# The end of a product ahead of the attention beside it, in the mixed units of a two-block transformer

## The reference, cut to what matters

```python
def first_block(x, mem, ...):
    x = x + hybrid_mixer(rmsnorm(x, g_mix), w_in, ...)      # 12 softmax heads and 4 stick-breaking heads
    x = x + memory_cross_attention(rmsnorm(x, g_cross), ...)
    x = x + squared_relu_mlp(rmsnorm(x, g_mlp), w_up, w_down)
    return rmsnorm(x, g_final)

def second_block(x, c, ctx, ...):
    for l in range(2):
        ...                        # latent stream x, and in layer 0 the context stream too:
        q_ctx = qk_heads(z_ctx[..., B_Q:B_K], q_norm_g[l])
        attn_ctx = diff_attention(q_ctx, k_ctx, v_ctx, lam)
        out_ctx = mixer_merge(z_ctx, attn_ctx, ...)   # branches a (spatial gate), b (attention), c (convolution)
        ctx = ctx + cg1 * out_ctx
        ...
```

## Time and profile before

| | us |
|---|---|
| median of 3 runs | 3848.04 (3846.48 to 3850.3) |
| profiled execution, device time | 3857.84 |
| its span, first to last instruction | 3856.0 |
| TensorE busy | 3587.3 (93%), 18826 matmuls |
| VectorE busy | 1574.4 (41%) |
| ScalarE busy | 961.7 (25%) |
| GpSimd busy | 2027.6 (53%) |
| granted TensorE clock, mean | 0.957 |

### The profile page before, as it was taken

The page is one execution under the profiler, slowest core; times in us unless marked ns, Lnnn a source line. Parts: engine busy times, 40 slices in busy tenths (PEclk is TensorE's granted clock), DMA queues, the critical chain, the costliest instruction groups (busy, mean ns, idle before and its releaser), DMA issues.

```text
span 3856.0 us, 47215 instructions
## 1 busy us (share of the span) xinstructions
PE 3587.3 (93%) x18826; PEld 2945.9 (76%) x18826; DVE 1574.4 (41%) x2738; ACT 961.7 (25%) x2038; POOL 2027.6 (53%) x1216
## 2 busy tenths in 40 slices
PE   8898889999899999899998899999999998999999
PEld 6776667787678998778776787888778766787887
DVE  7734442224864221464455313341472554214430
ACT  2134333222201111221244312220121443212210
POOL 4454245564458988745432364665544332465655
PEclk9899789988999999899999999999999999999999
DMA  8532122332664443332111132332322111232322
GB/s 297 169 119 82 49 70 84 110 104 66 219 207 131 143 142 121 119 116 72 66 55 44 55 95 80 94 98 90 108 72 77 55 55 44 71 93 82 97 86 101
DMA packets 109868, 389.26 MB, mean 101 GB/s; under 512 B 12057, under 2 KB 16537, under 8 KB 108242
## 3 DMA queue, kind: packets, MB, share of 16 engines
q1 hardware_dynamic: 89280, 315.10, 25.9%
q10 hardware_dynamic: 20370, 71.13, 5.4%
HBM read 379.86 MB, written 6.32 MB: 100 GB/s over the span
## 4 chain that ended last, share of the span: by engine, by line
PE 79%; DVE 13%; ACT 4%; issue 2%; DMA 1%; POOL 1%; ACTq 0%; DVEq 0%; SPq 0%
PE ps L319 20%; PE ps L321 19%; PE ps L320 19%; PE ps L1351 3%; DVE ada L1822 2%; DVE junk L1822 2%; PE ps L929 2%; PE ps L409 2%; PE ps L410 2%; PE ps L411 2%; PE ps L1363 1%; DVE ps L973 1%; DVE small_d L1408 1%; PE ps L1331 1%; PE ps L1044 1%
## 5 line engine op out<-in xcount | busy, mean ns | idle before, releaser
L2385 POOL CAST whi<-raw 128x1024 fp32r<-128x1024 f32 (+1 forms) x606 | 618.7, 1021 | 1767.8 <-DMA raw<-in_w 1767.2
L2387 POOL TENSOR_TENSOR wlo<-raw,whi 128x1024 fp32r<-128x1024 f32 (+1 forms) x606 | 1420.8, 2345 | 48.5
L319 PE MATMUL ps<-hhi,whi 128*128 128x512 f32 x2056 | 842.9, 410 | 90.9 <-DVE hlo L980 15.2
L320 PE MATMUL ps<-hlo,whi 128*128 128x512 f32 x2056 | 818.0, 398 | 0.0
L321 PE MATMUL ps<-hhi,wlo 128*128 128x512 f32 x2056 | 817.3, 398 | 0.0
L319 PEld LDWEIGHTS ps<-hhi,whi 128*128 128x128 f32 x2056 | 393.8, 192 | 211.3 <-DVE hlo L980 21.2
L320 PEld LDWEIGHTS ps<-hlo,whi 128*128 128x128 f32 x2056 | 395.2, 192 | 86.8 <-issue 6.7
L321 PEld LDWEIGHTS ps<-hhi,wlo 128*128 128x128 f32 x2056 | 393.9, 192 | 87.9
L319 PE MATMUL ps<-chi,whi 128*128 128x256 f32 x864 | 256.4, 297 | 6.6 <-DVE mc_lo L881 4.0
L320 PE MATMUL ps<-clo,whi 128*128 128x256 f32 x864 | 249.3, 289 | 0.0
L321 PE MATMUL ps<-chi,wlo 128*128 128x256 f32 x864 | 248.6, 288 | 0.0
(11 more groups left out here) (375 smaller groups left out, 6446.9 us busy)
## 6 DMA issues: line engine op xcount, KB each, us to landing
raw<-in_w SPq DMA_DIRECT2D x574, 512.0 KB, 3.6
ada<-in_ada ACTq DMA_DIRECT2D x96, 512.0 KB, 4.5
raw<-in_w SPq DMA_DIRECT2D x16, 384.0 KB, 3.4
att_toe<-toe_dram ACTq DMA_DIRECT2D x12, 256.0 KB, 3.1
raw<-in_w SPq DMA_DIRECT2D x16, 192.0 KB, 2.3
x<-in_x SPq DMA_DIRECT2D x4, 512.0 KB, 9.6
cond<-in_cc ACTq DMA_DIRECT2D x2, 1024.0 KB, 6.9
kc_dram<-kc ACTq DMA_DIRECT2D x2, 1024.0 KB, 4.9
```

Of the source, the lines that this page charges most:

```text
L319: nc.tensor.matmul(o, whi[:, buf, c], hi[:, k, 0:n], start=(k == 0), stop=False)
L320: nc.tensor.matmul(o, whi[:, buf, c], lo[:, k, 0:n], start=False, stop=False)
L2385: nc.gpsimd.tensor_copy(whi[:, buf, 0:c], raw[:, buf, 0:c]).then_inc(slab_hi, 1)
L2387: nc.gpsimd.tensor_tensor(wlo[:, buf, 0:c], raw[:, buf, 0:c], whi[:, buf, 0:c].bitcast(F32), ALU.subtract).then_inc(slab_split, 1)
```

## The change

The unit's first step of the third stream, if it is not a part's step 0, is split in two. `Products` keeps its faces `place` and `tensor` and stays where the step was. `Ends` has its faces `scalar` and `vector`, which belong to the tile before, and goes to the front of the unit, ahead of `first`. The steps in `some[1:]` are left whole.

```diff
+        class Ends(Part):
+            def __init__(self, part, i):
+                self.part, self.i = part, i
+            def scalar(self, act, _):
+                self.part.scalar(act, self.i)
+            def vector(self, dve, _):
+                self.part.vector(dve, self.i)
+
+        class Products(Part):
+            def __init__(self, part, i):
+                self.part, self.i = part, i
+            def place(self, _):
+                self.part.place(self.i)
+            def tensor(self, pe, _):
+                self.part.tensor(pe, self.i)
...
-            mixed = first + [attention.pop(0)] + second + norm[0:1] + some[0:1]
+            opened = []
+            if some and some[0][1]:
+                opened, some[0] = [(Ends(*some[0]), 0)], (Products(*some[0]), 0)
+            mixed = opened + first + [attention.pop(0)] + second + norm[0:1] + some[0:1]
             mixed += ([attention.pop(0)] if tiled[t] else []) + norm[1:2] + some[1:]
             for step in mixed:
                 place(*step)
```

## The result

| | before | after |
|---|---|---|
| median | 3849.07 us (4 runs, 3846.48 to 3850.3) | 3813.85 us (4 runs, 3805.17 to 3821.35) |
| profiled execution | 3857.84 us | 3821.35 us |
| its span | 3856.0 us | 3819.5 us |

The ratio is 0.9896, with a 95% interval of 0.9877 to 0.9914: 1.04% faster, 35 us between the medians and 36.5 between the two spans. The forecast was 3811 in a range of 3798 to 3831. The hit hides two terms that were wrong in opposite directions, and one that did not exist.

The account below looks back on a forecast made before the run. TensorE's queue, held by late ends of products, was taken as the bound. Waits net 24 us (29.5 - 1.4 - 4.4 + 0.9 - 0.6) plus clock 13 make 37 us: 3820.8 profiled, 3811 as median, range 3798 to 3831.

Parts of the forecast that it names:

- The bound: Units beside the context's attention: TensorE waits for late ends of products that still hold PSUM banks, 29.5 us.
- the 13 waits: TensorE's waits from 335 to 556 us for instructions reading a product out of PSUM; all 29.5 us go.
- The cover: Units 1 to 16: moved ends cost nothing, running while ScalarE and VectorE idle during the scores; uncovered, 0.4 us a unit.
- The table load: ScalarE's activation load at the unit's front falls in idle time; 0.6 us counted in all, a longer switch 0 to 4.
- Unit 5: The spatial gate's fourth group, moved ahead, delays the copy L1622, so TensorE waits 1.4 us more at L1606.
- The clock: Half-clock stretches behind the waits, 44.7 us, mostly return to full clock: 13 us gained, ends 0 and 19.
- Units 17 to 22: Conv ends at the front delay L1127, so TensorE waits in units 18, 20 and 21: 4.4 us lost, bounds 2 and 7.
- The clock doesn't come back: Rival: the waits go but half clock stays; gain 20 to 25 us, 3823 to 3828 us; chance 0.20.
- The next wait takes over: Rival: the fold or L1127 becomes as late as the bank was; gain 0 to 7 us, 3841 to 3848; chance 0.06.
- It doesn't do what it says: Rival: something else holds the moved end, so the bank comes no sooner; 3845 to 3850 us; chance 0.04.
- The slower one: Rival: moved ends delay the other softmax in units 18, 20, 21 and bring half clock; up to 3886 us; chance 0.04.

Follow-up runs that it names:

- the tiny addition out of the way: Changed kernel with the 128 x 1 addition of the sink as a tensor_scalar in place of a tensor_tensor: 0.9872 of the kernel before.
- the three restored waits: Changed kernel with ends at the front only in units 0 to 17, except units 7, 12 and 15: 0.9924 of the kernel before.
- the two runs with one part each: Changed kernel with ends at the front only in units 0 to 17, 0.9852 of the kernel before; only in units 18 to 22, 1.0038.

## Why the prediction was right, point by point

**The bound.** TensorE's queue, held by late ends: right. Each of the 13 waits is gone, and none came back under another name in units 0 to 16. The 29.5 us measured 30.4 as idle time, of which about 1.1 are shorter waits on the other softmax (3.7 before, 2.6 after).

**The cover.** Right in its result: in units 1 to 16 the moved ends cost TensorE nothing. One detail was wrong. The table load was said to carry no wait of its own. In unit 12 it does: `ACT_TABLE_LOAD` at 461.26 had stood idle for 1.17 us, waiting for the product, so the Tanh came 1.28 us later than the product's end allowed, and the copy L1646 stood behind it. TensorE did not feel it. The kernel before had shown such a load, in front of a Gelu:

```profile
346.38 1.28 ACT L486 ACT_TABLE_LOAD   x1 [4.37 <-PE ps L321]
```

The 0.6 us counted for this were not found. Nor was more than the load itself: in unit 12 the Tanh starts at 462.56, right behind the load's end at 462.54, and the estimate of 0 to 4 us for a longer switch came to nothing.

**Unit 5.** This term (1.4 us) does not exist. The prediction took L1606 to wait for the copy L1622 of the same unit. It uses the copy of the unit before: L1606 of step t works on pair t - 2, whose probabilities were copied in step t - 1. (Its own steps, added up, also give 408.5 and 1.3 us, not 408.55 and 1.4.) In the changed kernel's unit 5:

```profile
399.54 1.22 PE L1630 MATMUL ps<-vc,c_p 128*128 128x128 f32 x4
...
400.22 0.38 ACT L1646 ACTIVATE c_p<-ps 128x256 f32<-128x256 f32 x1
...
400.42 0.42 DVE L1795 TENSOR_TENSOR yac_lo<-ps,yac_hi 128x256 fp32r<-128x256 f32 x1 [0.52 <-ACT yac_hi L1762]
```

The copy (now L1646) is held up as foreseen, behind the gate's fourth group, and ends at 400.6. The value product (now L1630) had started at 399.54, without a wait.

**The clock.** The mechanism was right, the term too small: 13 us taken, 0 and 19 as ends, 23.7 measured in busy time of units 0 to 16, above the upper end. The count of half-clock stretches was short. The clock of 0.81 over 223.3 us means 2 x 0.19 x 223.3 = 85 us at 1.2 GHz, and 0.92 over 169.2 means 27 us: 58 us less, where eight stretches with 44.7 were counted. Times 44% that is 25.5, as measured within 2 us. The stretch at half speed with hardly any waits (441 to 457 in the kernel before) is gone too, so the third that was held back for it should not have been. In the changed kernel half clock is left only at the start of unit 0 and around the end of the gate's long wait and behind it; from there to the end of unit 16 the clock is full:

```profile
390.60:407.70 17.10, 15.13 (x51) 11.16 (x52) 9.83 (x26) 5.13 (x15) 3.63 (x3) 0.50 0.00 0
407.70:506.20 98.50, 96.47 (x581) 69.07 (x580) 58.42 (x185) 50.91 (x171) 35.91 (x22) 1.00 0.24 76
```

By the Trainium skill (page "TensorE: Matmul & The Clock Gate", Part 1), half of the throttled time, the 58 us would make 29, an estimate from that page; the measured 23.7 are nearer to the spacing's 44%.

**Units 17 to 22.** The mechanism was right and in the right units (18, 20, 21), the size wrong: 4.4 us taken (bounds 2 and 7), 9.7 measured, and 4.8 us of clock that were left out of the sum and appeared only in the rival that ended slower. With the tiny addition out of the way the waits were 2.0, 1.3 and 2.0, against the 1.7, 1.0 and 1.7 worked out. The rest is that one instruction, twice over 2 us. The profile of before had shown it: the same kind of addition (L1119) took 2.14 us ahead of TensorE's longest wait on L1127. It was mentioned as a bound and not priced. In the timeline of the kernel before, VectorE in unit 11, and TensorE's wait behind it (1.98 us):

```profile
485.01 2.14 DVE L1119 TENSOR_TENSOR small_s<-small_s 128x1 f32<-128x1 f32 x1
...
487.79 0.47 PE L1053 MATMUL ps<-cst,att_p 128*128 128x128 f32 x1 [1.98 <-DVE att_p L1127]
```

**The sum.** Forecast: 29.5 - 1.4 - 0.6 = 27.5 us of waits in units 0 to 16, 13 of clock, 4.4 - 0.9 = 3.5 lost in the units behind. Measured in the two profiled executions: 30.4, 23.7, 13.6 lost, and 4.0 lost outside the loop. 37 met 36.5 because the clock's return was too small by 11 us and the conv loss by 10. That the two sizes cancel is luck, and so is the close hit; each measured outside the bounds that its own term had (19 and 7). The range held for the same reason. The directions, the units and the mechanisms were right without luck, but for unit 5.

**The rivals.** "The clock doesn't come back" is out by the clock of 0.92 and by the three restored waits. "The next wait takes over" is out for units 0 to 16. In units 18, 20 and 21 waits on L1151 did come, but from the moved ends and not from TensorE being early, as the two runs with one part each show. "It doesn't do what it says" is out too, by the thirteen waits that went. The slower one named the right mechanism, and the part of the change for which it is true is slower by 0.4% when it stands alone.

## What to carry to other kernels

Where an engine's wait ends with an instruction that frees a buffer, look at what that instruction stood behind on its own queue. Put it ahead only where its engine would be idle until the same moment anyway, and leave it where the engine used that time for somebody else: here the one was worth 54 us and the other cost 14. When idle time of TensorE goes, price the clock with it, from the granted clock over the whole stretch and not from the pieces that catch the eye: here each microsecond of wait removed brought 0.5 to 0.8 more (5.9 on 12.7, 2.8 on 4.1, 23.7 on 30.4).

## What the runs showed of the hardware

A tensor_tensor of 128 x 1 elements in SBUF took up to 2.33 us while GpSimd ran a tensor_tensor of 128 x 1024 elements and up to 1.03 us while it ran a cast of that size, against 0.147 to 0.159 with GpSimd idle, and ended with the GpSimd instruction; the same sum as a tensor_scalar took 0.203 to 0.214 in all 16 places of each of two kernels.

An activation table load may run ahead of the wait of its activation or behind it. In the kernel before, ahead of unit 12's exponentials, it ran while the maximum that the exponential takes as its bias was still being made (L1653 on VectorE); the exponential began at 496.49, just behind it:

```profile
495.19 1.28 ACT L1630 ACT_TABLE_LOAD   x1
496.49 0.47 ACT L1630 ACTIVATE c_p<-ps,small_d 128x256 f32<-128x256 f32 x1
```

In the changed kernel the Tanh's load at 461.26 had waited for the product. So where a load is hidden has to be looked up in the timeline, not assumed.
